# GpSimd makes the low part of each weight chunk in four instructions of a quarter of the columns instead of one

## The chip, the core and the metric

One core of one Trainium2 chip. The time is that of one execution of the whole program on the device, in microseconds, as the median over runs. Before the change it is 2905.58 us (three runs, 2905.2 to 2906.4). One execution was recorded by the hardware profiler; all durations below come from that one.

## What is computed

Two stacked networks over 512 tokens of width 1024, all in float32:

- first block, two layers: `proj = rms_norm(x) @ w_in`; chunked attention with a relative bias over 8 heads of 64; chunkwise retention over 4 heads of 128 with rotary tables; `x + concat(ya*silu(ag), yr*silu(rg)) @ w_out`; at the end a final norm
- second block, two layers: `h + 0.5*swiglu_ffn(rms_norm(h))` (feed-forward of width 2816), then in the first layer a convolution module (a pointwise product, a sigmoid gate, 31 taps along the sequence, a layer norm, a second pointwise product) and in the second layer stick-breaking attention over 16 heads of 64 (`log_sigmoid`, a reversed cumulative sum, `exp`), then a second feed-forward, and at the end a final norm

Most of the work is dense products of a 1024 (or 2816) by 512 activation with weights that come from memory once.

## The kernel before, in words

**Precision.** A float32 product is made from three matmuls in the faster `float32r` form. Each operand is split into a high part (rounded) and a low part (the operand less its high part): `hi*hi`, `lo*hi` and `hi*lo` are summed in PSUM (`product`, lines 1266, 1267 and 1268).

**Weight stream.** All weights of the program are one stream of 220 chunks: 156 of 128 x 2048 and 64 of 128 x 1408 (the down projections of the feed-forwards). There are two slots, `s` = 0 and 1, and each of `raw`, `w_hi` and `w_lo` has both. A chunk goes through four stations: SyncE loads it into `raw` once the low part of the slot's last chunk is made (it waits for `lo_ready`, line 364 is the load); ScalarE rounds it into `w_hi` (`high_part`, line 558) once it has landed and the slot's last chunk has been multiplied (`chunk_done`); GpSimd subtracts and writes `w_lo` (`low_pair`, line 436) once `hi_ready` says so; TensorE waits for `lo_ready` and multiplies. So while TensorE works on chunk c, ScalarE and GpSimd in turn make chunk c+1, and the raw form of c+2 is on its way. The layers are `att_in`, `att_v`, `ret_in`, `ret_v` and `out` (twice), `up0`, `down0`, `pw1`, `pw2`, `up1`, `down1`, `k`, `v0`, `v1`, `up2`, `down2`, `q`, `o`, `up3` and `down3`.

**Activations.** Between layers VectorE scales the new `x` by a gain, rounds it to `x_hi` (line 814), makes `x_lo` (line 815, two inputs from SBUF), and adds up squares for the norm (line 829, two inputs from SBUF). TensorE's first chunk of a layer waits for these tile by tile, eight tiles of 128 features each. In the middle of that chunk TensorE sums the squares over features (line 1273), and at its end it makes a row of the norm (line 1280). The feed-forward's gate is applied and split on VectorE by lines 921 to 929.

**Attention and the rest.** In the attention stages VectorE, ScalarE and TensorE pass small tiles round: line 1014 adds the bias, 1030 scales the probabilities, 1429 transposes them. GpSimd copies heads into staging tiles (lines 461 to 465, and 522 to 526 for the stick-breaking stage, where VectorE splits with lines 1238 and 1239). In `pw1` GpSimd also builds the diagonal matrices of three of the eight feature tiles' taps (`taps_diag`, line 508) right behind each pair of low parts, and VectorE computes the taps of the other five by itself (line 1168, two inputs from SBUF).

**Order.** Every engine follows its own list of instructions, written out by hand; semaphores order them across engines. GpSimd's list around the change is: wait for `hi_ready`, subtract, signal `lo_ready`; the same for the other slot; then the next pair, or whatever staging copies stand between two layers.

Of the kernel before, what the change touches and what calls it, by code (L numbers as in the profile page):

```python
# [147 lines left out]
def build(nc, x_t, positions, vecs_d, bias_d, decay_d, w_feat, w_tok, w_out, w_up, w_down, w_pw1, w_pw2,  # L148
          w_k, w_v, w_q, w_o, out_t):
    f32, f32r, i32 = mybir.dt.float32, mybir.dt.float32r, mybir.dt.int32  # L150
    ALU, ACT, AX = mybir.AluOpType, mybir.ActivationFunctionType, mybir.AxisListType
# [3 lines left out]
    def sb(name, shape, dt=f32):  # L155
        return nc.alloc_sbuf_tensor(name, shape, dt)

    raw = sb("raw", [P, 2, CHUNK])
    w_hi = sb("w_hi", [P, 2, CHUNK], f32r)
    w_lo = sb("w_lo", [P, 2, CHUNK], f32r)  # L160
# [80 lines left out]
    def semaphore(name):  # L241
        return nc.alloc_semaphore(name)
# [3 lines left out]
    lo_ready = semaphore("lo_ready")  # L246
# [97 lines left out]
    def width(name):  # L344
        return DOWN_CHUNK if name.startswith("down") else CHUNK
# [82 lines left out]
    def _(pool):  # L428
        link = Tally(pool_link)

        def low_pair(name, i):
            w = width(name)
            for s in range(2):

                pool.wait_ge(hi_ready, first[name] + 2 * i + s + 1)
                nc.gpsimd.tensor_tensor(w_lo[:, s, 0:w], raw[:, s, 0:w], w_hi[:, s, 0:w].bitcast(f32),  # L436
                                        ALU.subtract).then_inc(lo_ready, 1)

        def low_parts(name):
            if phase_chunks[name] > 2:  # L440
                with pool.Fori(0, phase_chunks[name] // 2) as i:
                    low_pair(name, i)
            else:
                low_pair(name, 0)
# [54 lines left out]
        for n in range(2):  # L499
            low_parts(f"up{n}")  # L500
            low_parts(f"down{n}")
            if n == 0:

                pool.wait_ge(chunk_done, first["pw1"])
                for m, j in enumerate(CONV_ON_PE):
                    col0 = VCOL["w_dw"] + CONV_WIDTH * j
                    low_pair("pw1", m)
                    nc.gpsimd.tensor_tensor(
                        taps_diag[:, m, :, :], ident[:, :].unsqueeze(1).to_broadcast([P, CONV_WIDTH, P]),
                        vecs[:, col0:col0 + CONV_WIDTH].unsqueeze(2).to_broadcast([P, CONV_WIDTH, P]),  # L510
                        ALU.mult).then_inc(diag_ready, 1)
                low_pair("pw1", 3)
                low_parts("pw2")
# [1189 lines left out]
```

## Time and profile before

| | |
|---|---|
| median of three runs | 2905.58 us |
| lowest and highest | 2905.2, 2906.4 us |
| span of the profiled execution, first to last instruction | 2904.9 us |
| mean granted TensorE clock | 0.958 |
| busy: TensorE, VectorE, GpSimd, ScalarE | 2736.1, 1136.3, 995.4, 728.6 us |
| `w_lo` on GpSimd (line 436) | 220 instructions, 935.2 us busy |
| starts of two full matmuls in a row (1753.24 and 1753.48 us) | 0.23 us apart, so 1.4 us for the six of one feature tile |

No whole time of the profiled execution is given besides its span. The span is 0.3 us under the lowest of the runs and 0.7 us under their median, so what lies around it is that much, and a change of the span is read as the same change of the median. "Busy" counts the time in which an engine has an instruction under way, waiting for a port included. So the rows of a held-up instruction show a long duration and no idle time.

### The profile page before, as it was taken

To read this page: it belongs to the slowest core of one execution; us is meant where nothing else is said; L and a number is where in the kernel's file an instruction comes from. 1 tells how busy PE (TensorE), PEld (TensorE's weight loads), DVE (VectorE), ACT (ScalarE), POOL (GpSimd) and SP (SyncE) were. 2 spreads that over 40 slices of the span, in tenths; PEclk is the share of its full clock that TensorE was granted. 3 is DMA by queue.
4 is the path that set the end of the run, shared out by engine and by line. 5 is a ranking of instruction groups with operands and counts; after the bars stand their busy time and mean duration, and the time that the engine had idled before them with its cause. 6 is when DMAs were issued, how large, how long until landed. Compare 5 with 4: busy or idle time off the path is not lost.

```text
span 2904.9 us, 30751 instructions
## 1 busy us (share of the span) xinstructions
PE 2736.1 (94%) x11406; PEld 2097.0 (72%) x11406; DVE 1136.3 (39%) x1788; ACT 728.6 (25%) x922; POOL 995.4 (34%) x296
## 2 busy tenths in 40 slices
PE   7989899898799998978899999999999999999998
PEld 6647676476688887646788887778888755788886
DVE  3455532545522313794422321042231277432221
ACT  2332223322222222103222222222212355222221
POOL 3223232232244444410344444334434201344443
PEclk9889998899899999987999999999999999999999
DMA  4102221021122222200222223332222300222222
GB/s 166 44 29 102 73 87 44 30 102 45 69 89 101 83 90 88 73 29 1 87 87 101 88 90 102 126 116 94 94 90 99 116 0 15 73 88 99 92 90 79
DMA packets 38060, 230.10 MB, mean 79 GB/s; under 512 B 3936, under 2 KB 4064, under 8 KB 17504
## 3 DMA queue, kind: packets, MB, share of 16 engines
q1 hardware_dynamic: 37840, 226.97, 22.8%
q10 hardware_dynamic: 144, 2.10, 0.2%
q8 instruction: 51, 0.84, 0.1%
q14 instruction: 25, 0.20, 0.0%
HBM read 222.76 MB, written 6.29 MB: 79 GB/s over the span
## 4 chain that ended last, share of the span: by engine, by line
PE 81%; issue 11%; DVE 5%; POOL 2%; ACT 1%; DVEq 0%; POOLq 0%; ACTq 0%
PE ps L1266 24%; PE ps L1268 23%; PE ps L1267 23%; PE ps L1444 2%; PE ps L1603 2%; PE ps L1576 1%; POOL w_lo L436 1%; PE ps L1591 1%; PE ps L1419 1%; DVE x_lo L815 1%; PE ps L1429 1%; PE ps L1471 1%; DVE score L1030 1%; DVE score L1014 1%; DVE conv_out L1168 1%
## 5 line engine op out<-in xcount | busy, mean ns | idle before, releaser
L436 POOL TENSOR_TENSOR w_lo<-raw,w_hi 128x2048 fp32r<-128x2048 f32 (+1 forms) x220 | 935.2, 4251 | 1565.3 <-ACT w_hi L558 1556.0
L1266 PE MATMUL ps<-x_hi,w_hi 128*128 128x512 f32 x2304 | 913.7, 397 | 83.0 <-DVE x_lo L815 50.2
L1267 PE MATMUL ps<-x_lo,w_hi 128*128 128x512 f32 x2304 | 907.4, 394 | 0.0
L1268 PE MATMUL ps<-x_hi,w_lo 128*128 128x512 f32 x2304 | 906.8, 394 | 0.0
L1266 PEld LDWEIGHTS ps<-x_hi,w_hi 128*128 128x128 f32 x2304 | 439.7, 191 | 184.0 <-issue 59.0
L1268 PEld LDWEIGHTS ps<-x_hi,w_lo 128*128 128x128 f32 x2304 | 439.1, 191 | 92.9
L1267 PEld LDWEIGHTS ps<-x_lo,w_hi 128*128 128x128 f32 x2304 | 440.0, 191 | 91.0 <-issue 0.2
L558 ACT ACTIVATE w_hi<-raw 128x2048 fp32r<-128x2048 f32 (+1 forms) x220 | 385.1, 1750 | 429.0 <-PE ps L1268 423.8
L921 DVE TENSOR_TENSOR tmp<-ps,rms_b 128x512 f32<-128x512 f32 x88 | 60.9, 692 | 608.1 <-PE ps L1268 589.8
L1266 PE MATMUL ps<-hid_hi,w_hi 128*128 128x512 f32 x704 | 278.1, 395 | 0.0
L1268 PE MATMUL ps<-hid_hi,w_lo 128*128 128x512 f32 x704 | 278.1, 395 | 0.0
L1267 PE MATMUL ps<-hid_lo,w_hi 128*128 128x512 f32 x704 | 278.1, 395 | 0.0
L644 ACT ACTIVATE tmp<-tmp 128x512 f32<-128x512 f32 x88 | 55.8, 634 | 706.0 <-DVE tmp L921 705.9
L941 DVE SCALAR_TENSOR_TENSOR x<-ps,x 128x512 f32 x32 | 22.1, 692 | 389.3 <-PE ps L1268 389.3
L1268 PEld LDWEIGHTS ps<-hid_hi,w_lo 128*128 128x128 f32 x704 | 131.9, 187 | 32.4
L1266 PEld LDWEIGHTS ps<-hid_hi,w_hi 128*128 128x128 f32 x704 | 131.9, 187 | 32.3
L1267 PEld LDWEIGHTS ps<-hid_lo,w_hi 128*128 128x128 f32 x704 | 131.9, 187 | 32.3
L617 ACT ACTIVATE tmp<-x 128x512 f32<-128x512 f32 (+1 forms) x72 | 45.5, 632 | 352.0 <-DVE x L941 236.8
L829 DVE TENSOR_TENSOR sq_sum<-sq_sum,tmp 128x512 f32<-128x512 f32 x80 | 82.0, 1025 | 25.8 <-ACT tmp L617 24.8
L1512 PE MATMUL ps<-conv_in,taps_diag 128*128 128x512 f32 x186 | 81.8, 600 | 9.3 <-ACT conv_out L747 9.3
L929 DVE TENSOR_TENSOR hid_lo<-tmp,hid_hi 128x512 f32 x88 | 84.9, 964 | 10.8
L815 DVE SCALAR_TENSOR_TENSOR x_lo<-x,vecs,x_hi 128x512 fp32r<-128x512 f32 (+1 forms) x72 | 78.9, 1096 | 4.8
(174 smaller groups left out, 2331.7 us busy)
## 6 DMA issues: line engine op xcount, KB each, us to landing
raw<-in_w_up SPq DMA_DIRECT2D x88, 1024.0 KB, 4.9
raw<-in_w_down SPq DMA_DIRECT2D x64, 704.0 KB, 4.0
raw<-in_w_feat SPq DMA_DIRECT2D x24, 1024.0 KB, 4.9
raw<-in_w_pw SPq DMA_DIRECT2D x12, 1024.0 KB, 4.9
raw<-in_w_tok SPq DMA_DIRECT2D x8, 1024.0 KB, 4.9
raw<-in_w_out SPq DMA_DIRECT2D x8, 1024.0 KB, 4.9
bias<-in_bias_t SPq DMA_DIRECT2D x2, 2048.0 KB, 9.7
raw<-in_w_k SPq DMA_DIRECT2D x4, 1024.0 KB, 4.8
```

The costliest lines, as they stand in the source:

```text
L436: nc.gpsimd.tensor_tensor(w_lo[:, s, 0:w], raw[:, s, 0:w], w_hi[:, s, 0:w].bitcast(f32), ALU.subtract).then_inc(lo_ready, 1)
L558: nc.scalar.activation(w_hi[:, s, 0:w], raw[:, s, 0:w], ACT.Copy).then_inc(hi_ready, 1)
L815: nc.vector.scalar_tensor_tensor(out=x_lo[:, j, :], in0=x[:, j, :], scalar=g, in1=x_hi[:, j, :].bitcast(f32), op0=ALU.mult, op1=ALU.subtra ...
L829: nc.vector.tensor_tensor(sq_sum[:, :], sq_sum[:, :], tmp[:, slot, :], ALU.add)\
L921: nc.vector.tensor_tensor(tmp[:, s, :], ps[:, 2 * s, :], rms_b[:, :], ALU.mult)\
L929: nc.vector.tensor_tensor(hid_lo[:, j, :], tmp[:, 2 + s, :], hid_hi[:, j, :].bitcast(f32), ALU.subtract).then_inc(hidden_ready, 1)
L1266: nc.tensor.matmul(out, hi, src_hi, start=start, stop=False, skip_group_check=True)
L1267: nc.tensor.matmul(out, hi, src_lo, start=False, stop=False, skip_group_check=True)
L1268: return nc.tensor.matmul(out, lo, src_hi, start=False, stop=stop, skip_group_check=True)
L1444: ins = nc.tensor.matmul(ps[e:e + ATT_DIM, 4 + s, P * kt:SEQ], v_st[:, s, kt, e:e + ATT_DIM], source[:, kt, P * kt:SEQ], start=kt == 0, st ...
L1512: ins = nc.tensor.matmul(ps[:, 4 + m % 2, :], taps_diag[:, m, tap, :], conv_in[:, CONV_ON_PE[m], tap:tap + SEQ], start=tap == 0, stop=tap ...
L1603: ins = nc.tensor.matmul(ps[:, Z_BANK[u % ROUND], P * (r - later):SPAN[r]], weights[:, :], part[:, head % 2, at], start=False, stop=later ...
```

## The change

Where GpSimd makes the low part of a chunk in slot `s`, the one subtraction over all `w` columns (2048 or 1408) becomes four, over a quarter each (512 or 352). The wait for `hi_ready` stands ahead of the first alone, and `lo_ready` is signalled by the fourth alone. Nothing else is touched: no buffer, no semaphore, no order of the work.

```diff
             for s in range(2):
 
                 pool.wait_ge(hi_ready, first[name] + 2 * i + s + 1)
-                nc.gpsimd.tensor_tensor(w_lo[:, s, 0:w], raw[:, s, 0:w], w_hi[:, s, 0:w].bitcast(f32),
-                                        ALU.subtract).then_inc(lo_ready, 1)
+                for at in range(0, w, w // 4):
+                    part = slice(at, at + w // 4)
+                    ins = nc.gpsimd.tensor_tensor(w_lo[:, s, part], raw[:, s, part],
+                                                  w_hi[:, s, part].bitcast(f32), ALU.subtract)
+                ins.then_inc(lo_ready, 1)
```

## Rows read from the trace of the kernel before

**Rows 1.** The page: the span, and the chain that ended last, by engine.
```profile
span 2904.9 us, 30751 instructions
...
PE 81%; issue 11%; DVE 5%; POOL 2%; ACT 1%; DVEq 0%; POOLq 0%; ACTq 0%
```

**Rows 2.** Waits of TensorE: us in total, times, longest us.
```profile
PE ps L1266 <- DVE x_lo L815: 50.2, 14, 13.9
PE ps L1266 <- POOL w_lo L436: 23.1, 5, 10.5
```

**Rows 3.** Timeline at 380 us: start us, us taken, instruction [idle before <-releaser].
```profile
380.23 4.82 POOL L436 TENSOR_TENSOR w_lo<-raw,w_hi 128x2048 fp32r<-128x2048 f32 x1 [6.26 <-ACT w_hi L558]
...
380.70 4.90 DVE L815 SCALAR_TENSOR_TENSOR x_lo<-x,vecs,x_hi 128x512 fp32r<-128x512 f32 x1
385.52 0.47 DVE L814 TENSOR_SCALAR x_hi<-x,vecs 128x512 fp32r<-128x512 f32 x1
...
385.65 0.50 PE L1266 MATMUL ps<-x_hi,w_hi 128*128 128x512 f32 x1 [2.34 <-DVE x_lo L815]
```

**Rows 4.** Timeline at the start of pw1, GpSimd, VectorE, TensorE.
```profile
1128.58 9.20 POOL L436 TENSOR_TENSOR w_lo<-raw,w_hi 128x2048 fp32r<-128x2048 f32 x2 [9.29 <-PE ps L1268]
1137.73 7.28 POOL L508 TENSOR_TENSOR taps_diag<-ident,vecs 128x3968 f32<-128x3968 f32 x1
...
1129.51 3.86 DVE L814 TENSOR_SCALAR x_hi<-x,vecs  x1 [0.16 <-DVE x L941]
1133.49 4.84 DVE L815 SCALAR_TENSOR_TENSOR x_lo<-x,vecs,x_hi  x1
1138.25 7.31 DVE L829 TENSOR_TENSOR sq_sum<-sq_sum,tmp 128x512 f32<-128x512 f32 x1
...
1145.61 1.87 PE L1273 MATMUL ps<-ones,sq_sum 128*128 128x1 f32 x8 [2.95 <-DVE sq_sum L829]
```

**Rows 5.** Timeline of GpSimd: the same taps instruction with no VectorE turn ahead of it.
```profile
1173.54 6.83 POOL L508 TENSOR_TENSOR taps_diag<-ident,vecs 128x3968 f32<-128x3968 f32 x1
```

**Rows 6.** Timeline: undisturbed low parts, two copies in a row, TensorE's start on a chunk.
```profile
59.03 4.60 POOL L436 TENSOR_TENSOR w_lo<-raw,w_hi 128x2048 fp32r<-128x2048 f32 x1 [6.97 <-ACT w_hi L558]
...
163.13 0.61 POOL L462 COPY k_st<-qk 128x512 f32<-128x512 f32 x1
163.69 0.61 POOL L465 COPY v_st<-v_tok 128x512 f32<-128x512 f32 x1
...
1748.97 3.23 POOL L436 TENSOR_TENSOR w_lo<-raw,w_hi 128x1408 fp32r<-128x1408 f32 x1 [6.00 <-ACT w_hi L558]
...
1753.48 0.40 PE L1266 MATMUL ps<-hid_hi,w_hi 128*128 128x512 f32 x1
```

**Rows 7.** Windows at 1145 us: stretch, busy us of PE, PEld, DVE, ACT, POOL, PEclk.
```profile
1145.00:1152.00 7.00, 6.39 (x19) 5.40 (x20) 0.74 (x2) 0.26 (x1) 0.01 (x1) 0.51 0.00 0
```

**Rows 8.** Timeline in the first layer's attention: GpSimd and VectorE.
```profile
164.26 4.68 POOL L436 TENSOR_TENSOR w_lo<-raw,w_hi 128x2048 fp32r<-128x2048 f32 x1
...
165.55 3.47 DVE L1030 TENSOR_SCALAR score<-score,small 128x128 f32<-128x128 f32 x1
...
170.86 0.34 DVE L1030 TENSOR_SCALAR score<-score,small 128x256 f32<-128x256 f32 x1
```

**Rows 9.** Timeline of VectorE in the stick-breaking stage.
```profile
2438.73 4.04 DVE L1238 CAST soft_hi<-tmp 128x128 fp32r<-128x128 f32 x1
```

**Rows 10.** Timeline of VectorE in the convolution.
```profile
1225.33 5.00 DVE L1168 SCALAR_TENSOR_TENSOR conv_out<-conv_in,vecs,conv_out  x1
1230.25 0.74 DVE L1168 SCALAR_TENSOR_TENSOR tmp<-conv_in,vecs,tmp 128x512 f32<-128x512 f32 x1
```

**Rows 11.** Timeline at the third chunk of up0: GpSimd, VectorE, TensorE.
```profile
780.62 4.50 POOL L436 TENSOR_TENSOR w_lo<-raw,w_hi 128x2048 fp32r<-128x2048 f32 x1 [22.76 <-ACT w_hi L558]
...
782.52 3.15 DVE L927 TENSOR_TENSOR tmp<-tmp 128x512 f32<-128x512 f32 x1 [2.20 <-ACT tmp L644]
...
785.17 0.80 PE L1266 MATMUL ps<-x_hi,w_hi 128*128 128x512 f32 x1 [7.06 <-POOL w_lo L436]
```

## The prediction

> **What bounds the kernel now.** I read the chain that ended last first: TensorE holds 81% of it, VectorE 5%, GpSimd 2% [rows 1]. So nothing that GpSimd does counts by itself; it counts where TensorE stands still for it, or for somebody it holds up. The waits of TensorE name both kinds: 50.2 us for `x_lo`, which VectorE makes, and 23.1 us in five places for `w_lo` itself [rows 2]. The timeline says why `x_lo` is late. At 380.70 it takes 4.90 us, and the step normally ends and begins again in under 1 us; GpSimd's `w_lo` runs from 380.23 to 385.05, and `x_lo` ends 0.55 us after it [rows 3]. One of the two engines holds something that the other needs, for a whole instruction. (The Trainium skill, SBUF — State Buffer, "SBUF: two separate sides", calls it a port pair that is locked exclusively for the full instruction; the trace agrees, with the 4.90.)
>
> **Does a queue of GpSimd instructions let VectorE in between?** The whole change hangs on this, and one stretch shows it. At 1128.58 two `w_lo` follow each other without a pause (9.20 us together) and `taps_diag` follows them. `x_hi` waits through the first, ends at 1133.37, `x_lo` waits through the second, ends at 1138.33, and `sq_sum` waits through the third, ends at 1145.56 [rows 4]. So at each boundary exactly one waiting VectorE instruction gets its turn. Its price for GpSimd: `taps_diag` takes 7.28 us behind `x_lo` and 6.83 where no VectorE instruction took a turn ahead of it, so 0.45 a turn [rows 4, 5].
>
> **The cost of a quarter.** Undisturbed low parts take 4.60 us for 2048 columns and 3.23 for 1408 [rows 6]: 2.14 ns a column and 0.22 fixed. Two copies of 0.61 us start 0.56 apart [rows 6], so 0.05 of the fixed part overlaps, and an extra instruction costs 0.17. Three make a chunk 0.5 us longer; a quarter of 2048 is 1.32 us, started every 1.27. Bounds: nothing at the low end (the two sizes show that the cost isn't proportional, so no gain), and at the high end 0.56 each, if all of a copy's spacing were fixed. I take 0.17, as it comes from the same operation. The Trainium skill (GPSIMD Engine Reference, "Elementwise — side-by-side cycle accounting") gives 2.6 cycles an element at 1.2 GHz and 4497 ns for this form, which leaves 0.06 fixed; by it the five gating chunks would lose next to nothing, and the sum would be some 2 us better.
>
> **What hides the 0.5.** In the tightest steady state, the second chunk of each pair in a down projection, `w_lo` ends at 1752.20 and TensorE starts on it at 1753.48: 1.28 us of slack [rows 6], seen 32 times; elsewhere it is 1.3 to 3 us. Without that cover 32 chunks would pay what is over. SyncE's next load starts 0.5 later behind `lo_ready`; it has the whole of another chunk's product to land in. The wait for `hi_ready` is not moved and nothing new is queued behind it.
>
> **The gains, place by place.**
> 1. Splits of `x` at the start of a layer: the place at 380 and three like it (at 1421, 1890 and 2521). With quarters `x_lo` of the second tile is done at 382.3, not 385.6. But the next `x_hi`, `x_lo` meet the next quarters: every turn is 1.3 of GpSimd and 0.1 to 0.45 of VectorE, so the third tile ends at 385.4 (was 386.8) and the fourth at 387.6 (was 388.0). TensorE needs 1.4 per tile. Its last start after a wait was 385.65 with seven tiles to go [rows 3], and becomes 387.65 with five to go: 0.7 us each, 2.8. A fifth place, at 753, has four such VectorE steps a tile and gets 0.2. Most of the 4 us of hold-up is handed out again in portions, and only where VectorE has little to do is it saved.
> 2. Attention, once in each layer: a `score` tile of 128 columns that should take 0.3 is held 3.47 us by the `w_lo` of 164.26, and the ring VectorE, ScalarE, TensorE stands still. It asks at 165.55, the first quarter ends at about 165.6. If it gets that boundary it saves 3.2, if it just misses it, 2.1; the next two such steps (1.9 us later [rows 8], and 0.8 after that) meet later quarters and give back 0.7. So 1.4 to 2.5; I take 2.0 each, 4.0.
> 3. The start of `pw1`: `x_hi`, `x_lo` and `sq_sum` take the first three boundaries of the first low part and are done at 1133.5, where `sq_sum` ended at 1145.56. TensorE starts 1.4 later than 1133.3, since the low part with three turns in it ends at 1134.6, but no longer stops for the sum of squares at 1145.61 (a wait of 2.95 [rows 4]): 1.7 net. After that stop its granted clock is 0.51 for the window from 1145 to 1152, the 1.2 GHz level, and 18 matmuls and the row take until 1154: about 2.2 us more than at the upper level [rows 7]. With the stop gone I count that back: 3.9.
> 4. Stick-breaking stage: `soft_hi` of 128 columns is held 4.04 us [rows 9]; quarters leave 0.8, and the next three steps meet more quarters: 1.2 net.
> 5. Convolution: VectorE's taps are the bound and each needs the port. A tap is held 5.00 us, free ones start 0.66 apart [rows 10]. In turns, four taps cost 4 x (1.27 + 0.45) = 6.9 where one held tap and three free ones take 7.0. With the 0.1 that the first overlaps, 0.2 each for four low parts: 0.8.
> 6. The start of the program, where both `x_hi` and a squares' sum are held: 0.7 gained, 0.5 lost at the third chunk, 0.2 net.
>
> **The losses.** Five chunks gate TensorE [rows 2]. Those of the start and of `pw1`'s start are in the sums above. `pw1`'s last one gets 1.8 longer, but VectorE bounds that stage. `pw2`'s second loses 0.5. At `up0`'s third TensorE waits from 778 for a `w_lo` of 4.50, and VectorE's gate step at 782.52, held 3.15 us, now gets in, and two more behind it [rows 11]: 0.5 for the quarters and 0.6 for the turns, 1.1. GpSimd's staging copies in retention come 0.5 later; there the gain of one turn pays for it.
>
> Sum: 2.8 + 0.2 + 4.0 + 3.9 + 1.2 + 0.8 + 0.2 - 0.5 - 1.1 = 11.5 us. The span goes from 2904.9 to 2893.4; runs stand 0.7 above it, so the median goes to 2894.1.
>
> **The rivals.**
> A. *No boundary inside a run of GpSimd instructions.* The four quarters carry no wait between them; the boundary at 1133 did, though its wait was met before. If GpSimd keeps its hold, VectorE waits as before, and five chunks pay 0.5: 2908, within the bound of what can be told. Against it: the boundary between `w_lo` and `taps_diag` carries no wait either, and `x_lo` got in [rows 4]. The Trainium skill (GPSIMD Engine Reference, "Instruction dispatch") says that GpSimd's cores start the next instruction without waiting for each other, by which such a gap might never open; that is this rival.
> B. *The hold-up is only handed out differently.* What VectorE needs in a stretch and what GpSimd needs in it add up either way. If attention misses its boundary twice (-1.2), the clock stays low after `pw1`'s start anyway (-2.2), splits give 0.2 each (-2) and `up0`-like losses double (-1), 5 us are left: 2901. For it: my own working of the splits and the convolution. Against it: attention and stick-breaking have one short step held by a long one.
> C. *The fixed cost breaks the cover; slower.* Place: the 32 chunks with 1.28 us of slack, of which 0.1 is the signal. Point: 0.4 us per extra instruction. At 0.56 [rows 6] a chunk grows by 1.7 and each stalls 0.5, 16 us; four gating chunks pay 1.2 more than counted, 5; gains of 10 remain: about 2905.6 + 16 + 5 - 10 = 2917. Against it: the two sizes of the very same operation allow 0.22.
>
> **How the numbers follow.** About 0.2% (5.8 us) is what a measurement of this kernel can tell from no change. Forecast 0.74, A 0.06, B 0.13, C 0.07. The forecast lies on the faster side, A and B within the bound, C slower: 0.74, 0.19, 0.07. Range: at the good end an extra instruction costs nothing (2.4 more), attention gets both boundaries (1.0) and the clock comes back earlier at two splits too (3.5): 2887. At the other end it takes in B with half its gain lost again: 2903. A and C lie outside.
>
> **What would show it.** `x_lo` of line 815: longest 4.9 now, then under 2 us, with several of 1.3 to 2 in its place. `soft_hi` and `score` likewise. GpSimd: 880 instructions of 1.0 and 1.3 us at line 436, busy time up by about 110 us (220 x 0.5). TensorE's wait for `x_lo` falls from 50 to about 40 us in more pieces, that for `sq_sum` at `pw1` is gone; its wait for `w_lo` rises by 3 to 4. The down projections keep their pace. I am wrong if a `w_lo` quarter takes over 1.6 us alone, if a VectorE instruction is still held 4 us, or if the down projections get slower.

## The result and the profile after

The changed kernel takes 2924.65 us (median of 4 runs, 2922.16 to 2925.28) where the kernel before takes 2905.99 (4 runs, 2905.20 to 2906.52): a ratio of 1.0061 with a 95% interval of 1.0048 to 1.0074. It is 18.7 us slower, where 11.5 us of gain were forecast. The prediction has the wrong sign, and the result lies outside its range.

The page of the changed kernel, with its span, its engines, the row of TensorE's granted clock in 40 slices of 73 us, and the chain that ended last:

```profile
span 2922.8 us, 31411 instructions
...
PE 2765.7 (95%) x11406; PEld 2110.4 (72%) x11406; DVE 1052.3 (36%) x1788; ACT 728.5 (25%) x922; POOL 1124.9 (38%) x956
...
PEclk9889998999899999987999999999999679999999
...
PE 82%; issue 10%; DVE 5%; POOL 3%; ACT 1%; DVEq 0%; POOLq 0%; ACTq 0%
```

VectorE is busy for 84 us less than before (1136.3 then), nearly all of it time in which an instruction had begun and was held. The chain has hardly moved against [rows 1]. What is new is a 6 and a 7 in the clock row, at slices 32 and 33. The same row of the kernel before has a 9 in both:

```profile
PEclk9889998899899999987999999999999999999999
```

The waits of TensorE after the change (us in total, times, longest us), which answer to [rows 2]:

```profile
PE ps L1269 <- POOL w_lo L438: 41.9, 6, 14.4
PE ps L1269 <- DVE x_lo L818: 30.0, 16, 5.0
PE ps L1432 <- DVE score L1033: 18.3, 21, 1.6
```

`w_lo` and `x_lo` together cost 71.9 us, against 73.3 before; one long wait at the start has only changed its name, since `x_lo` (13.9, last to come before) now comes ahead of `w_lo` (14.4). The wait for `score` fell from 22.6 to 18.3 us. So the waits are somewhat better, and the loss isn't among them.

The low parts of the changed kernel, by form (times, then busy us, mean ns of one, idle time before):

```profile
L438 POOL TENSOR_TENSOR w_lo<-raw,w_hi 128x512 fp32r<-128x512 f32 x624 | 827.8, 1357 | 1158.8 <-ACT w_hi L561 1149.9 <-PE ps L1271 8.9
L438 POOL TENSOR_TENSOR w_lo<-raw,w_hi 128x352 fp32r<-128x352 f32 x256 | 237.6, 960 | 273.3 <-ACT w_hi L561 273.3
```

They add up to 1065.4 us, where the 220 whole ones took 935.2: 130 more, 110 of which were forecast.

**Where the time went.** I lined the traces up by TensorE's first matmul on each chunk of weights. Up to the second chunk of `up2` in the third feed-forward the changed kernel is ahead by 13.02 us. The first row is the kernel before, the second the changed one:

```profile
1902.52 0.39 PE L1266 MATMUL ps<-x_hi,w_hi 128*128 128x512 f32 x1
...
1889.50 0.39 PE L1269 MATMUL ps<-x_hi,w_hi 128*128 128x512 f32 x1
```

The stick-breaking stage starts 13.0 us earlier too (first product 2289.52, was 2302.53), and there it turns round. From its first product to its last it took 169.6 us before and takes 202.3 after: 32.7 more. After it the changed kernel is 19.7 behind, and it ends 17.9 behind. The windows of that stage (stretch, its us, busy us of PE, PEld, DVE, ACT, POOL with counts, PEclk, DMA share, GB/s), the kernel before first:

```profile
2300.00:2305.00 5.00, 3.42 (x14) 1.81 (x12) 2.23 (x6) 0.62 (x2) 0.00 (x0) 1.00 0.00 0
2305.00:2319.00 14.00, 14.00 (x37) 8.22 (x37) 8.38 (x22) 5.40 (x13) 0.00 (x0) 0.52 0.01 2
2319.00:2400.00 81.00, 81.00 (x319) 42.47 (x318) 57.01 (x136) 44.02 (x98) 7.67 (x12) 1.00 0.00 0
```

And the changed kernel:

```profile
2287.00:2292.00 5.00, 3.42 (x13) 1.69 (x11) 2.23 (x6) 0.62 (x2) 0.00 (x0) 0.96 0.00 0
2292.00:2380.00 88.00, 88.00 (x198) 44.99 (x197) 38.03 (x92) 27.14 (x62) 3.72 (x6) 0.50 0.00 1
2380.00:2400.00 20.00, 20.00 (x79) 10.38 (x79) 12.87 (x31) 11.67 (x25) 1.92 (x3) 0.99 0.00 0
```

Both run up to the stage with the same pauses (3.42 of 5 us busy), and in both the granted clock then falls to 0.50, the 1.2 GHz level. Before, it is back at the 2.4 GHz level after 14 us. After the change it stays down for 88 us, with 198 matmuls in a stretch in which the upper level does some 350. PE reads 88.00 of 88 busy both ways: a busy share of 100% says nothing of the rate, only the clock column and the count do. GpSimd makes no low part of weights in the changed kernel's windows from 2292 on; its 6 instructions of 3.72 us are copies that stage heads. The change isn't at work in this stage; the stage is only entered 13 us sooner.

The place at which the clock falls differs, counted from the stage's first product. The kernel before keeps the upper level until 3.0 us behind it, and the changed one until 2.1 us behind it:

```profile
2302.53:2305.50 2.97, 2.97 (x10) 1.70 (x11) 1.34 (x5) 1.07 (x4) 0.00 (x0) 1.00 0.00 0
2305.50:2306.50 1.00, 1.00 (x2) 0.00 (x0) 0.59 (x2) 0.38 (x1) 0.00 (x0) 0.51 0.00 0
```

```profile
2289.52:2291.60 2.08, 2.08 (x8) 1.22 (x8) 0.54 (x3) 0.62 (x2) 0.00 (x0) 1.00 0.00 0
2291.60:2292.60 1.00, 1.00 (x4) 0.39 (x2) 0.80 (x4) 0.56 (x2) 0.00 (x0) 0.51 0.00 0
```

### The profile page after: what moved, and what is told of

Read it like the earlier page. It is cut to its first block, busy times and chain, and to the rows that moved or that the text cites. A ratio compares the mean times of both kernels' runs of the same rounds, so it can differ in the third digit from the quotient of the medians.

```text
span 2922.8 us, 31411 instructions
## 1 busy us (share of the span) xinstructions
PE 2765.7 (95%) x11406; PEld 2110.4 (72%) x11406; DVE 1052.3 (36%) x1788; ACT 728.5 (25%) x922; POOL 1124.9 (38%) x956
## 4 chain that ended last, share of the span: by engine, by line
PE 82%; issue 10%; DVE 5%; POOL 3%; ACT 1%; DVEq 0%; POOLq 0%; ACTq 0%
PE ps L1269 23%; PE ps L1270 23%; PE ps L1271 23%; POOL w_lo L438 3%; PE ps L1606 2%; PE ps L1579 2%; PE ps L1447 2%; PE ps L1594 2%; PE ps L1422 1%; DVE x_lo L818 1%; PE ps L1432 1%; PE ps L1474 1%; PE ps L1582 1%; DVE tmp L1171 1%; DVE score L1017 1%
## 5 line engine op out<-in xcount | busy, mean ns | idle before, releaser
L438 POOL TENSOR_TENSOR w_lo<-raw,w_hi 128x512 fp32r<-128x512 f32 (+1 forms) x880 | 1065.4, 1241 | 1432.1 <-ACT w_hi L561 1423.2
L1269 PE MATMUL ps<-w_hi,x_hi 128*128 128x512 f32 x192 | 74.8, 390 | 2.5 <-ACT sb_v L657 2.5
L1270 PE MATMUL ps<-w_lo,x_hi 128*128 128x512 f32 x192 | 74.7, 389 | 0.0
L1271 PE MATMUL ps<-w_hi,x_lo 128*128 128x512 f32 x192 | 74.7, 389 | 0.0
```

The source lines that it names most:

```text
L438: ins = nc.gpsimd.tensor_tensor(w_lo[:, s, part], raw[:, s, part], w_hi[:, s, part].bitcast(f32), ALU.subtract)
L1269: nc.tensor.matmul(out, hi, src_hi, start=start, stop=False, skip_group_check=True)
L1270: nc.tensor.matmul(out, hi, src_lo, start=False, stop=False, skip_group_check=True)
L1271: return nc.tensor.matmul(out, lo, src_hi, start=False, stop=stop, skip_group_check=True)
```

## The experiments

Two theories stood at first. Theory 1: the stage's clock depends on when it is entered, and any shift could do this, in the kernel before too. Theory 2: the quarters ahead of the stage (of `q`, whose chunk is being made just before) disturb its start.

**The quarters of q taken away**

```diff
-                for at in range(0, w, w // 4):
-                    part = slice(at, at + w // 4)
+                pieces = 1 if name == "q" else 4
+                for at in range(0, w, w // pieces):
+                    part = slice(at, at + w // pieces)
```

> Quarters everywhere except in the layer q, the last one ahead of the stick-breaking stage. Theory 1 (the stage is slow because TensorE's granted clock stays at the lower level from its start, and that depends on when and in what rhythm the stage starts, not on any quarter near it): TensorE's times up to the stage are those of the changed kernel, so the stage stays slow: about 2924, with some 85 us at a granted clock of 0.5. Theory 2 (the quarters of q, which run just before the stage, disturb its start): the stage is as before, and the gain of 13 us that stood before it is kept: about 2891.

2924.77 us (2922.34 to 2924.97, 4 runs), ratio 1.0063 [1.0046, 1.0080]. The window of the stage:

```profile
2292.00:2380.00 88.00, 88.00 (x198) 44.87 (x197) 38.46 (x94) 27.14 (x62) 3.71 (x6) 0.50 0.00 1
```

Nothing changed. Theory 2 falls.

**Quarters in q and o alone** (`pieces = 4 if name in ("q", "o") else 1`)

> Quarters in the layers q and o alone, whole instructions everywhere else. Theory 1: TensorE starts the stick-breaking stage at the same time as in the kernel before, with the clock as before; about 2904 to 2906, less 1 to 2 for the low part of o that holds VectorE up. Theory 2 (the quarters of q disturb the stage): about 2936.

2905.75 us (2904.62 to 2909.04, 10 runs), ratio 1.0003 [0.9994, 1.0013]; the stage takes 169.0 us with 13.7 at the lower level. The quarters nearest to the stage do no harm without the shift.

**The changed kernel with TensorE kept at work where the stage begins.** The fillers are matmuls whose product nobody reads.

```diff
+        def filler(n):
+            for _ in range(n):
+                nc.tensor.matmul(ps[:, 6, :], x_hi[:, 7, 0:P], x_hi[:, 7, :], start=True, stop=True,
+                                 skip_group_check=True)
...
+        filler(8)
         def sb_products(step, i):
+            if 1 <= step <= 4 and isinstance(i, int) and i == 0:
+                filler(6)
```

> The changed kernel with 32 filler matmuls of TensorE at the start of the stick-breaking stage (8 before its first product, 6 behind each of the next four; they write a bank that nobody reads), so that TensorE doesn't thin out there. Theory 1: the granted clock stays at the upper level or comes back soon, the stage takes about what it took before or less, about 2890 to 2896 with 2 to 4 us paid for the fillers. If the clock stays low whatever TensorE does in those microseconds, about 2927 to 2931.

2894.89 us (2891.39 to 2895.15, 5 runs), ratio 0.9958 [0.9944, 0.9972]. The windows at the same place:

```profile
2287.00:2292.00 5.00, 3.53 (x16) 2.60 (x15) 1.29 (x2) 0.00 (x0) 0.00 (x0) 1.00 0.01 3
2292.00:2380.00 88.00, 88.00 (x351) 47.89 (x350) 59.89 (x146) 45.01 (x101) 5.77 (x9) 1.00 0.00 0
```

The clock never falls in the stage, 351 matmuls fit into the same 88 us, and the stage takes 168.7 us. The time lost was the clock's, all of it.

**The same fillers in the kernel before**

> The kernel before with the same fillers. Theory 1: the 14 us at the lower clock at the stage's start go away or shrink (worth up to 7 us) and 2 to 4 us are paid: 2900 to 2908. If fillers only cost time: 2908 to 2911.

2907.78 us (2906.12 to 2910.01, 10 runs), ratio 1.0008 [0.9999, 1.0018]; the stage 169.3 us, none of it at the lower level. Here the fillers cost what they give back. So the 12.9 us between this run and the last are the quarters' effect, with the clock of this stage equal in both. The clock elsewhere still has a part in them: over the whole span 238.5 us are at the lower level here and 227.3 in the run before.

**The kernel before, entering the stage later.** Theory 1 has two forms: the stage's place against the steps of the clock decides ("phase"), or something that quarters change in the last microseconds ahead of it ("rhythm"). Four or eight of the same matmuls stand between `up2` and `down2`, some 180 us ahead of the stage, and nothing else is changed:

```diff
+        filler(4)
```

> The kernel before, with 4 filler matmuls of TensorE (0.23 us each, 0.9 in all) between the layers up2 and down2, some 180 us ahead of the stick-breaking stage; no quarters anywhere. Theory 1, phase: the changed kernel's stage stood 0.9 us otherwise to the clock's own steps than the stage before did, and that alone decides; the stage here falls as it falls in the changed kernel, takes about 202 us and the program about 2939. Theory 1, rhythm: it is something in the last microseconds ahead of the stage that quarters change: the stage takes 169 to 170 and the program 2907.

2941.21 us (2939.15 to 2943.27, 2 runs), ratio 1.0122 [1.0092, 1.0152]. The windows of the stage:

```profile
2303.00:2308.00 5.00, 3.42 (x14) 2.02 (x13) 1.82 (x5) 0.62 (x2) 0.00 (x0) 1.00 0.00 0
2308.00:2397.00 89.00, 89.00 (x200) 45.31 (x199) 38.45 (x94) 27.39 (x63) 3.72 (x6) 0.50 0.00 1
```

There is not one quarter in this kernel, and it has the changed kernel's loss to within a microsecond: the stage takes 202.9 us, 88.7 of them at the lower level. Four matmuls that nobody needs, far ahead of the stage, make the kernel 1.2% slower, in both of its two runs.

> The same with 8 fillers, 1.8 us. Phase: another place again, so the length of the stage may be 169, 202 or between, and differs from that of 4 fillers or of none in the time at the lower clock. Rhythm: 2907.5 with the stage at 169 to 170.

With eight it is 2907.56 us (2906.18 to 2911.18, 8 runs), ratio 1.0007 [0.9996, 1.0019], and the stage takes 171.1 us:

```profile
2304.00:2322.00 18.00, 18.00 (x44) 9.75 (x42) 9.32 (x25) 6.89 (x17) 0.00 (x0) 0.53 0.01 1
```

With more matmuls in the same place the loss is gone again: it comes and goes with them. The time of entry by itself isn't what decides. Traces of one and the same code differ by some microseconds already ahead of these matmuls (the one with four stood 2.5 us behind the kernel before there, after a stretch at the lower level behind the convolution that lasted 37.5 us instead of 34.1), and none of the 57 runs of the kernel before, from 2903.3 to 2909.6 us, has the loss. What moves with the matmuls is the distance from the stage's first product to the fall of the clock: 3.0 us with none, 2.2 with four (0.9 us of work), 1.2 with eight (1.8 us).

**The changed kernel, entering the stage later** (`filler(11)` at the same place)

> The changed kernel with 11 such fillers (2.5 us) between up2 and down2, which puts its stage where the stage of the kernel before stood to the clock's steps. Phase: the stage takes 169 to 170 us with about 14 at the lower clock, and the program about 2893 to 2895. Rhythm: the stage keeps its 202 us, the program about 2927.

2893.29 us (2892.02 to 2893.74, 4 runs), ratio 0.9958 [0.9938, 0.9978]:

```profile
2295.00:2309.00 14.00, 14.00 (x37) 8.08 (x36) 7.98 (x20) 5.05 (x13) 0.00 (x0) 0.51 0.00 1
2309.00:2390.00 81.00, 81.00 (x320) 42.73 (x319) 57.49 (x137) 43.95 (x98) 7.69 (x12) 1.00 0.00 0
```

The changed kernel with more work is 31 us faster than without it. All its quarters are there, and the stage starts at 2292.00, 2.5 us later. The clock's fall stands 3.0 us behind the first product again, as in the kernel before. With this theory 1 stands from both sides, in the form of the phase: the kernel before can be given the loss, and the changed one can be rid of it, by a delay alone.

**Fillers in the stage and a delay ahead of it**

> The changed kernel with the fillers at the stage's start and 4 more between up2 and down2. If fillers at the start make the stage's clock safe, 0.9 us of shift costs 0.9 us: about 2895.5, the stage 169 us. If they only moved it to a lucky place: 30 us more, about 2927.

2893.71 us (2891.14 to 2894.64, 4 runs), ratio 0.9958 [0.9942, 0.9975]; the stage 168.7 us, nothing at the lower level. With fillers this second moment of entry makes no difference; a delay like this had cost the kernel before 35 us.

**The size of the pieces**, all with the stage's fillers: halves, then eighths.

> Two halves instead of four quarters, with the fillers at the stage's start. A chunk grows by 0.14 instead of 0.43 us, a held VectorE step waits up to 2.3 instead of 1.3 us. The gating chunks and the turns on them lose less, the attention tiles save less: 2891 to 2897, the same as with quarters within what can be told.

2898.87 us (2893.83 to 2900.76, 10 runs), ratio 0.9975 [0.9966, 0.9985]. That is outside the 2891 to 2897 that I expected. Halves seem to give less than quarters, though the interval just overlaps that of quarters (0.9944 to 0.9972). Against the trace with quarters and fillers they lose 1.0 us in the first attention, 1.9 at `up0`'s third chunk, 1.5 in the convolution's taps (with 0.9 gained just ahead of them) and 1.6 in `v1`, where the clock falls once more, and gain 2.1 at the start of `pw1`. A held `score` of 128 columns takes 1.20 us there, where quarters leave 0.28.

> Eight pieces, with the fillers. A chunk grows by 7 x 0.14 = 1.0 us and more VectorE steps get a turn on it; the tightest down chunks keep 0.3 us of slack. Gating chunks lose 3 to 5 us more than with quarters, attention gains up to 1: 2896 to 2901. If the fixed cost were hidden behind the piece before: 2893.

2887.41 us (2885.22 to 2889.37, 4 runs), ratio 0.9939 [0.9923, 0.9956]. I expected eighths to be slower than quarters, and they are faster by some 6 to 7 us: the slowest of the four runs is below the fastest of the nine with quarters and the stage's fillers (2891.14), though the intervals of the ratios overlap a little. A chunk in eighths:

```profile
39.90 5.57 POOL L439 TENSOR_TENSOR w_lo<-raw,w_hi 128x256 fp32r<-128x256 f32 x8 [13.68 <-ACT w_hi L562]
```

An undisturbed chunk takes 4.60 us whole [rows 6], 4.74 in halves, 5.02 in quarters and 5.58 in eighths. Each further instruction costs 0.14, and still the down projections don't stall, whose chunks go from 3.23 to 4.22 within 1.28 of slack. Against quarters, eighths gain 1.7 us in each attention and 0.5 to 1.2 in each split of `x`. At the start they gain 1.2 and give more than that back before the first attention. They lose 2.3 at `up0`'s third and fourth chunks and 1.8 at `pw1`'s sixth, which the taps of the convolution then win back. Some of their lead is the clock's again: 211 us of the span are at the lower level, 227 with quarters.

**Quarters only where they gained**: `att_in1`, `ret_in0`, `ret_in1`, `up1`, `up2`, `up3`, `o` and the first pair of `pw1`, whole elsewhere.

> Quarters only where the trace shows a VectorE step held up on TensorE's path (att_in1, ret_in of both layers, up1, up2, up3, o and pw1's first pair), whole instructions where the low part itself gates TensorE (att_in0, up0, pw2, pw1's last pair) and elsewhere; with the fillers. Keeps the gains and drops the losses of the start (1.3), up0 (1.6) and pw2 (0.4): 2890 to 2892, the best of all. If the losses were made up elsewhere: 2894 as with quarters everywhere.

2891.45 us (2887.61 to 2895.55, 4 runs), ratio 0.9952 [0.9936, 0.9969]. Its interval overlaps that of quarters everywhere (0.9944 to 0.9972), so these runs don't settle that leaving them out is worth anything. Its trace loses 1.6 us in `v1` at a fall of the clock that the traces with quarters everywhere don't have, so the clock is mixed into this comparison too.

**The best version found**: eighths, but `up0` and `pw2` whole, with the stage's fillers.

```diff
-                nc.gpsimd.tensor_tensor(w_lo[:, s, 0:w], raw[:, s, 0:w], w_hi[:, s, 0:w].bitcast(f32),
-                                        ALU.subtract).then_inc(lo_ready, 1)
+                pieces = 1 if name in ("up0", "pw2") else 8
+                for at in range(0, w, w // pieces):
+                    part = slice(at, at + w // pieces)
...
```

> Eight pieces everywhere except in up0 and pw2, whose low parts gate TensorE with VectorE little held up, with the fillers at the stage's start. Against eighths everywhere this drops what the pieces cost at up0's second and third chunk and at pw2's second, 3 to 4 us: 2884, from 2882 to 2887. If those losses were made up later in the same layers: 2887, as with eighths everywhere.

2885.10 us (2883.00 to 2887.21, 5 runs), ratio 0.9933 [0.9920, 0.9947], faster than both kernels: some 20 us under the kernel before, and some 40 under the changed one. Its waits of TensorE:

```profile
span 2881.3 us, 32172 instructions
...
PE ps L1275 <- POOL w_lo L439: 46.4, 9, 16.1
PE ps L1275 <- DVE x_lo L819: 24.7, 12, 5.0
```

TensorE waits for `w_lo` in nine places, six with quarters: eighths bring GpSimd nearer to being the bound. From eighths everywhere (0.9923 to 0.9956) the intervals don't tell it apart.

## Why the prediction was wrong, step by step

**The step that failed** stands in no line of the sum, and that is the fault. The text counted the clock at one place, the start of `pw1`, and took every stage that the change doesn't touch at its old duration. The page had the warning: 246 us of the span before were at the lower level, and the stick-breaking stage began with 13.7 of them. The runs showed that the length of this stage is set by how its start falls against the clock: 169.6 us before and 202.3 after, with 13.7 and 88.7 us at the lower level. The rivals had no such case; the clock stood in B as 2.2 us and in the range as 3.5, where 32.7 came. Of the sum, then:

**GpSimd lets VectorE in at each boundary: right.** The place of [rows 3], after:

```profile
376.93 6.37 POOL L438 TENSOR_TENSOR w_lo<-raw,w_hi 128x512 fp32r<-128x512 f32 x4 [5.84 <-ACT w_hi L561]
...
377.40 1.65 DVE L818 SCALAR_TENSOR_TENSOR x_lo<-x,vecs,x_hi 128x512 fp32r<-128x512 f32 x1
378.96 1.50 DVE L817 TENSOR_SCALAR x_hi<-x,vecs 128x512 fp32r<-128x512 f32 x1
380.50 1.66 DVE L818 SCALAR_TENSOR_TENSOR x_lo<-x,vecs,x_hi 128x512 fp32r<-128x512 f32 x1
382.08 1.51 DVE L817 TENSOR_SCALAR x_hi<-x,vecs 128x512 fp32r<-128x512 f32 x1
...
382.21 0.50 PE L1269 MATMUL ps<-x_hi,w_hi 128*128 128x512 f32 x1 [0.68 <-DVE x_lo L818]
```

Four VectorE instructions go through a chunk in turns, where one was held for all of it. The longest `x_lo` fell from 4.91 to 1.66 us, and the chunk takes 6.37 instead of the 5.02 of an undisturbed one: 1.35 for its turns, 0.45 for each of three. Rival A falls with this: VectorE gets in between two instructions that nothing separates. (The Trainium skill, SBUF — State Buffer, "SBUF: two separate sides", has the holder keep the pair for the whole instruction; the trace agrees in that no held step here is longer than one quarter and its own time.) The one step of VectorE that GpSimd still holds for long in the changed kernel, a tap of 7.32 us at 1187.90, stands behind a `taps_diag` of 7.28 us, which is not cut up.

**How far a figure by place can be trusted.** What follows compares one trace with one trace. Four more traces hold the same code as the kernel before up to `up2` (quarters in `q` and `o` alone, and the kernel before with the stage's fillers, with four and with eight matmuls). With quarters up to there, five traces exist in all. Among those without quarters the start up to the third chunk differs by up to 1.3 us, the first attention by 2.1, the second by 1.4, `att_in1`'s split by 2.4 and a retention stage with its `out` by 1.4 to 2.7. From `up0` to `up2` they agree within 0.2, but for the one stretch of 37.5 us at the lower level.

**The splits: right in kind, too small in size.** 0.7 each was forecast for four. Measured are 0.6 at `att_in1`, and 3.2, 2.3 and 2.3 at `up1`, `up2` and `up3`. The other traces without quarters take 1.6 to 2.4 us longer at `att_in1` than the one that I worked from, so against the mean of the five the gain there is 2.2 as well. In these places part of the gain is again the clock (at `up1` it is at the lower level for 13.7 us before and 6.8 after); I haven't parted the two. VectorE's own times at `att_in1` came out as worked: counted from the chunk's start, the second and third tiles' `x_lo` end after 2.1 and 5.2 us, as forecast.

**Attention: right in kind, too small in the first layer.** 2.0 for each layer was forecast, from a held `score` step and 0.7 given back. Measured are 4.7 us in the first (3.2 with the fillers of the later stage, in another execution) and 3.0 in the second; by the means of five traces without quarters and five with, 3.0 and 2.1. The rows that answer to [rows 8]:

```profile
164.18 5.20 POOL L438 TENSOR_TENSOR w_lo<-raw,w_hi 128x512 fp32r<-128x512 f32 x4
...
165.46 0.28 DVE L1033 TENSOR_SCALAR score<-score,small 128x128 f32<-128x128 f32 x1
167.62 0.62 DVE L1033 TENSOR_SCALAR score<-score,small 128x256 f32<-128x256 f32 x1
168.68 0.91 DVE L1033 TENSOR_SCALAR score<-score,small 128x384 f32<-128x384 f32 x1
```

The first boundary was met, and the next two steps give back 0.28 and 0.5, as counted on VectorE. The fault is that I charged them to the path. The transposes of TensorE in the timeline of the kernel before, and then of the changed one:

```profile
169.08 0.47 PE L1429 MATMUL ps<-ident,score 128*128 128x128 f32 x1 [2.74 <-DVE score L1030]
...
171.26 0.69 PE L1429 MATMUL ps<-ident,score 128*128 128x128 f32 x2 [0.98 <-DVE score L1030]
```

```profile
168.30 0.52 PE L1432 MATMUL ps<-ident,score 128*128 128x128 f32 x2 [1.37 <-DVE score L1033]
```

Two waits became one of 1.37, and the products behind them begin 3.1 us earlier (168.75, was 171.88). Most of the rest of the first layer's 4.7 lies ahead of the held step: the lead grows by 1.3 us between 100 and 152 us, where the clock is at the lower level for 17.1 us in place of 20.5.

**The start of pw1: right.** Forecast 3.9. Its first chunk comes 1.5 later and its second 5.7 earlier, 4.2 net. The three VectorE steps of [rows 4] take the first boundaries, and the stop at the sum of squares is gone:

```profile
1122.52 10.95 POOL L438 TENSOR_TENSOR w_lo<-raw,w_hi 128x512 fp32r<-128x512 f32 x8 [8.87 <-PE ps L1271]
1133.43 6.82 POOL L511 TENSOR_TENSOR taps_diag<-ident,vecs 128x3968 f32<-128x3968 f32 x1
...
1123.45 0.62 DVE L817 TENSOR_SCALAR x_hi<-x,vecs  x1 [0.17 <-DVE x L944]
1124.19 1.55 DVE L818 SCALAR_TENSOR_TENSOR x_lo<-x,vecs,x_hi  x1
1125.67 1.75 DVE L832 TENSOR_TENSOR sq_sum<-sq_sum,tmp 128x512 f32<-128x512 f32 x1
...
1128.79 0.76 PE L1269 MATMUL ps<-x_hi,w_hi 128*128 128x512 f32 x1 [6.35 <-POOL w_lo L438]
```

**The stick-breaking stage's held step: right in kind, half the size, and drowned.** The `soft_hi` of 4.04 us [rows 9] takes 0.76 after, and two steps behind it take 1.26 and 1.38. On TensorE the stage gains 0.6 us, where 1.2 was forecast: 169.0 against 169.6 with the short fall of the clock in both, and 168.7 against 169.3 with fillers in both.

**The convolution: right on VectorE, given back on TensorE.** Two taps in turns start 1.69 apart (1.72 was assumed), and TensorE's last taps begin 11.1 us earlier than before, on a lead of 10.3 at the stage's start: 0.8, as forecast:

```profile
1214.86 1.76 DVE L1171 SCALAR_TENSOR_TENSOR conv_out<-conv_in,vecs,conv_out  x1
1216.55 1.75 DVE L1171 SCALAR_TENSOR_TENSOR tmp<-conv_in,vecs,tmp 128x512 f32<-128x512 f32 x1
```

But the stretch at the lower level that follows lasts 41 us, 34 before, and takes back 3.1. It is the failed step in small: the kernel before with four matmuls, which has no quarter, loses 3.2 at the same place with 37.5 us.

**Start, `up0` and `pw2`.** The start was to gain 0.2 and lost 1.3 (0.4 in the run with fillers): the first chunk in quarters took 6.01 us with its turns, not 4.50. But the kernel before with four matmuls, which has no quarter, stands 1.3 behind there too, so no gain or loss is told at this place. `up0`'s second and third chunks lose 0.6 and 1.0, and the fourth wins 0.9 back; 1.1 was the forecast. `pw2`'s second loses 0.4, forecast 0.5. Each retention stage loses 0.3, behind the staging copies, which the text had taken as paid for; against the mean of the five it is more, some 1.2 with its `out`, and why isn't shown.

**The fixed cost: right.** 0.17 was assumed, 0.14 measured:

```profile
41.92 5.02 POOL L438 TENSOR_TENSOR w_lo<-raw,w_hi 128x512 fp32r<-128x512 f32 x4 [17.03 <-ACT w_hi L561]
...
1769.03 3.66 POOL L438 TENSOR_TENSOR w_lo<-raw,w_hi 128x352 fp32r<-128x352 f32 x4 [5.58 <-ACT w_hi L561]
```

The down projections keep their pace, with the slack down from 1.28 to 0.85 us; rival C falls. GpSimd's busy time rises by more than 110 because turns are inside it.

**The sum.** Up to the stick-breaking stage the forecast had 10.3 us (11.5 less 1.2, the step inside it), and 13.0 came; by the means of the five traces on either side, without the added matmuls, it is 11.8. With the clock of that stage put right the changed kernel takes 2893 to 2895 us, which is where the forecast of 2894.1 stood. But these two kernels carry matmuls that the forecast didn't have. Like with like, the change is worth 12.9 us (fillers on both sides) or 14.4 (the 2.5 us of the eleven matmuls taken off), each known to some 4 us, where 11.5 were forecast. Rival B, 5 us in all, is not what happened. That the total comes so near is partly luck: in the pair of traces attention and the splits gave 9.3 us more than was counted, and the stretch at the lower level behind the convolution, the start, retention and the stage's own step gave less or took some back. The likeliest time was thus a fair account of the queues and a wrong forecast of the kernel: the change itself is worth some 13 to 14 us, and the moment at which it made the stick-breaking stage begin cost 33.

What goes with the length is known, and the reason is not. In the three traces with 88.7 us at the lower level (the changed kernel, the one with `q` whole, the kernel before with four matmuls) the clock falls 2.1 to 2.2 us behind the stage's first product. In the three with 13.7 (the kernel before, quarters in `q` and `o` alone, the changed kernel with eleven matmuls) it falls 3.0 to 3.1 us behind it, and in the one with 17.1 it is 1.2. TensorE is busy for 3.42 of the last 5 us ahead of the fall in all seven. Why a fall at 2.1 us keeps the clock down for more than six times as long as one at 3.0 isn't shown by any row. In the three long cases the clock comes back at the same place of the stage, 90.8 to 90.9 us behind its first product; why there, no run tells.

## What to carry to other kernels

Before pricing a change, mark every stretch of the clock row that lies below the upper level, also far from the change, and give "this stretch gets longer or shorter because it starts at another moment against the clock" a rival and a place in the range. Where a run contradicts a sum that the waits bear out, compare stages by matmuls per microsecond, not by busy share, and shift the old kernel by a few harmless instructions to see whether it has the same fault. An instruction that holds something a short one needs is worth cutting up, as long as its engine has slack for the fixed cost of each piece.

## What the runs showed of the hardware

- GpSimd and VectorE hand over at every boundary of back-to-back GpSimd instructions, one waiting VectorE instruction at each. A turn costs GpSimd about 0.45 us between the `x_hi` and `x_lo` steps of 512 columns (a chunk of 6.37 us for 5.02), and less for short ones (three turns in a chunk of 5.51 us in the stick-breaking stage).
- A further GpSimd instruction of this kind costs 0.14 us net (a chunk takes 4.60, 4.74, 5.02 and 5.58 us in one, two, four and eight).
- One and the same stage took 169.6 or 202.3 us by how its start fell against the clock, with the same instructions in the same order. It stayed at the 1.2 GHz level for 88.7 us while PE read as busy throughout. In the kernel before, four further matmuls ahead of it (the stage began at 2305.93 instead of 2302.53) brought this about, and eight (2303.05) did not. The clock fell 2.1 to 2.2 us behind the stage's first product in the three long cases, and 3.0 to 3.1 or 1.2 us behind it in the four short ones.
- 32 matmuls that fill the pauses at its beginning kept the clock up in all seven kernels that had them, at entries from 2281.8 to 2301.9 us. They cost about what a short fall of the clock costs: 2907.8 with them and 2906.0 without, in the kernel before.
